# Gathering the tokens of two experts at once, with 256-column one-hot matrices on tokens split beforehand

## The reference

```
logits = h @ w_router                                  # 8 experts
top_val, top_idx = top_k(logits, 2)
gates = sum(one_hot(top_idx, 8) * softmax(top_val)[..., None], axis=-2)
out = 0
for e in range(8):
    out += gates[..., e:e+1] * ((silu(h @ w_gate[e]) * (h @ w_up[e])) @ w_down[e])
```

## Time and profile before

| | us |
|---|---|
| median of 3 runs | 1962.38 (1959.33 to 1962.86) |
| the profiled execution's own time | 1953.69 |
| its span, first to last instruction | 1951.5 |
| TensorE busy | 1850.6 |
| VectorE busy | 1636.3 |
| ScalarE busy | 1139.7 |

### The profile page before, as it was taken

How to read it: one execution, slowest core, us unless ns; L and a number is a source line. 1 busy time by engine, 2 the same in 40 slices (tenths; PEclk the granted TensorE clock), 3 DMA queues, 4 the chain that set the end, 5 groups by cost and what they waited for, 6 DMA issues and landing times.

```text
span 1951.5 us, 32205 instructions
## 1 busy us (share of the span) xinstructions
PE 1850.6 (95%) x10670; PEld 1595.1 (82%) x10670; DVE 1636.3 (84%) x2193; ACT 1139.7 (58%) x1616; POOL 36.1 (2%) x47
## 2 busy tenths in 40 slices
PE   3999999989999999999999999978899999889997
PEld 2989998867788888888888888866789997679997
DVE  6999996868998899898989898988897768897554
ACT  2445444464777777777777777753654445555443
POOL 2000000000000000000000000000000000000000
PEclk8999999999999999999999999989899999899999
DMA  9978996657899999999999999958678885855772
GB/s 323 349 270 289 385 372 182 175 178 248 266 343 359 347 357 345 356 353 348 362 336 371 330 371 331 370 181 243 189 227 283 276 262 185 231 194 188 224 226 76
DMA packets 368485, 551.26 MB, mean 282 GB/s; under 512 B 35827, under 2 KB 293110, under 8 KB 368342
## 3 DMA queue, kind: packets, MB, share of 16 engines
q1 hardware_dynamic: 365392, 547.81, 83.6%
q10 hardware_dynamic: 2118, 1.46, 0.3%
q0 software_dynamic: 832, 0.30, 0.1%
HBM read 548.38 MB, written 1.08 MB: 282 GB/s over the span
## 4 chain that ended last, share of the span: by engine, by line
PE 81%; DVE 13%; issue 3%; ACT 2%; DMA 1%; DVEq 0%; ACTq 0%; SPq 0%
PE ps L448 23%; PE ps L446 23%; PE ps L447 23%; DVE mod_acc L1768 2%; DVE units_low L441 2%; PE ps L1226 2%; PE ps L959 1%; DVE prob L1962 1%; PE ps L1101 1%; DVE x_tokens L1795 1%; DVE x_normed L1794 1%; PE ps L971 1%; DMA mod_in<-in_mod_w 1%; PE ps L806 1%; PE ps L781 1%
## 5 line engine op out<-in xcount | busy, mean ns | idle before, releaser
L441 DVE TENSOR_TENSOR units_low<-raw_units,units_high 128x1024 fp32r<-128x1024 f32 (+1 forms) x838 | 982.5, 1218 | 129.9 <-ACT units_high L437 127.2
L437 ACT ACTIVATE units_high<-raw_units 128x1024 fp32r<-128x1024 f32 (+1 forms) x838 | 846.1, 1058 | 292.0 <-PE ps L448 251.5
L446 PE MATMUL ps<-units_high,hT_high 128*128 128x512 f32 (+1 forms) x992 | 391.3, 394 | 2.7 <-DVE hT_low L2196 1.4
L448 PE MATMUL ps<-units_high,hT_low 128*128 128x512 f32 (+1 forms) x992 | 389.8, 393 | 0.0
L447 PE MATMUL ps<-units_low,hT_high 128*128 128x512 f32 (+1 forms) x992 | 386.8, 390 | 0.0
L446 PE MATMUL ps<-hT_high,units_high 128*128 128x256 f32 x1152 | 319.1, 277 | 4.2 <-DVE hT_low L1837 3.0
L447 PE MATMUL ps<-hT_low,units_high 128*128 128x256 f32 x1152 | 318.5, 276 | 0.0
L448 PE MATMUL ps<-hT_high,units_low 128*128 128x256 f32 x1152 | 318.4, 276 | 0.0
L446 PE MATMUL ps<-units_high,aT_high 128*128 128x512 f32 x632 | 255.2, 404 | 1.3 <-DVE aT_low L2048 0.6
L448 PE MATMUL ps<-units_high,aT_low 128*128 128x512 f32 x632 | 248.7, 394 | 0.0
L447 PE MATMUL ps<-units_low,aT_high 128*128 128x512 f32 x632 | 247.1, 391 | 0.0
(11 more groups left out here) (304 smaller groups left out, 1605.2 us busy)
## 6 DMA issues: line engine op xcount, KB each, us to landing
raw_units<-in_moe_w_gate SPq DMA_DIRECT2D x352, 256.0 KB, 4.6
raw_units<-in_moe_w_up SPq DMA_DIRECT2D x352, 256.0 KB, 5.8
raw_units<-in_moe_w_down SPq DMA_DIRECT2D x176, 512.0 KB, 6.1
mod_in<-in_mod_w SPq DMA_DIRECT2D x96, 512.0 KB, 6.4
mod_in<-in_w_mod SPq DMA_DIRECT2D x96, 512.0 KB, 5.6
raw_units<-in_w_gu SPq DMA_DIRECT2D x176, 256.0 KB, 3.9
raw_units<-in_w_down SPq DMA_DIRECT2D x44, 512.0 KB, 4.1
raw_units<-in_w_in SPq DMA_DIRECT2D x32, 512.0 KB, 7.6
```

The source lines that it names most:

```text
L437: eng.activation(whi[:rows, high_slot(f, n), 0:width], raw[:rows, raw_slot(f, n), 0:width], ACT.Copy).then_inc(f.hi, 1)
L441: eng.tensor_tensor(low[:rows, raw_slot(f, n), 0:width], raw[:rows, raw_slot(f, n), 0:width], whi[:rows, high_slot(f, n), 0:width].bitcast ...
L446: pe.matmul(dst, ah, bh, start=start, stop=False, **kw)
L448: return pe.matmul(dst, al, bh, start=False, stop=stop, **kw)
```

## The change

The tokens are split once, in expert 0 (ScalarE `tokens_high` and VectorE `tokens_low` at its steps 5 and 7), into `xth` and `xtl`. `hot` becomes a matrix of 256 columns in fp32r. Expert 1 and 2, 3 and 4, 5 and 6 and, at the end of expert 6, 7 and the one behind it are gathered together by `gather_pair`. Expert 0 keeps a gather of its own in float32. `hTh` and `hTl` hold two experts side by side, the even one in columns 128 to 255, the odd one in 0 to 127 (`slots`). The pair's result lies in banks 2, 3, 5 and 7 and is evicted in four parts. The bodies of the three loops hold an even and an odd expert: experts 0 and 1 are straight code, and the loop makes three turns. SP's program is unchanged. The diff, cut to its core:

```diff
-    hot = ex("gather_hot", [P, T, P])
+    hot = ex("gather_hot", [P, T, 2 * P], F32R)
+    xth = ex("tokens_high", [P, T, D], F32R)
+    xtl = ex("tokens_low", [P, T, D], F32R)
+    GATHER_BANKS = (2, 3, 5, 7)
+    def slots(odd):
+        return slice((1 - odd) * P, (2 - odd) * P)
...
     # TensorE
-        def gather(value, halves=False):
-            pe.wait_ge(s_hot, value)
-            for c in range(DC):
-                for t in range(T):
-                    last = pe.matmul(ps[:, 2 + c // 4, (c % 4) * P:(c % 4 + 1) * P], xn[:, t, c * P:(c + 1) * P],
-                                     hot[:, t, :], start=t == 0, stop=t == T - 1)
+        def gather_pair(it):
+            pe.wait_ge(s_xth, T)
+            pe.wait_ge(s_xtl, T)
+            pe.wait_ge(s_hot, it + 2 * T)
+            pe.wait_ge(s_hTe, it + 2)
+            for c in range(DC):
+                dst = ps[:, GATHER_BANKS[c // 2], (c % 2) * 2 * P:(c % 2 + 1) * 2 * P]
+                for t in range(T):
+                    pe.matmul(dst, xth[:, t, c * P:(c + 1) * P], hot[:, t, :], start=t == 0, stop=False)
+                    last = pe.matmul(dst, xtl[:, t, c * P:(c + 1) * P], hot[:, t, :], start=False, stop=t == T - 1)
+                if c % 2 == 1:
+                    last.then_inc(s_gat, 1)
...
-            swiglu(fa, N_MOE, STEPS, 1, it, first=[(s_xel, it + 2), (fa.act, STEPS + STEPS * it)],
-                   hooks={("after_T", 1): scat0, ("after_T", 2): scat1, ("after_T", 3): hot_T,
-                          ("before_T", STEPS): lambda: gather(it + 2)})
-        expert(0)
-        with pe.Fori(1, E) as it:
-            expert(it)
+            hooks = {("after_T", 1): scat0, ("after_T", 2): scat1, ("after_T", 3): hot_T}
+            if not odd:
+                hooks["before_T", STEPS] = lambda: gather_pair(it)
+            swiglu(fa, N_MOE, STEPS, 1, it, first=[(s_xel, 2 * it + (4 if odd else 2)), (fa.act, STEPS + STEPS * it)],
+                   hooks=hooks, at0=slots(odd).start)
+        expert(0, 0)
+        expert(1, 1)
+        with pe.Fori(2, E - 1, 2) as it:
+            expert(it, 0)
+            expert(it + 1, 1)
...
     # ScalarE
-        def xe_high(v):
-            ac.wait_ge(s_gat, v + 1)
-            ac.activation(hTh[:, 0:DC, 0:P], ps[:, 2:4, :].rearrange("p a (c s) -> p (a c) s", c=4), ACT.Copy)\
-                .then_inc(s_xeh, 1)
+        def xe_high(it):
+            for q in range(4):
+                ac.wait_ge(s_gat, 2 * it + 3 + q)
+                ac.activation(hTh[:, 2 * q:2 * q + 2, :].rearrange("p c s -> p (c s)"), ps[:, GATHER_BANKS[q], :],
+                              ACT.Copy).then_inc(s_xeh, 1)
+        def tokens_high(t):
+            ac.activation(xth[:, t, :], xn[:, t, :], ACT.Copy).then_inc(s_xth, 1)
+            if first:
+                hooks[5], hooks[7] = (lambda: tokens_high(0)), (lambda: tokens_high(1))
+            if not odd:
+                hooks[STEPS] = lambda: xe_high(it)
...
     # VectorE
+        def xe_low(it):
+            for q in range(4):
+                ve.wait_ge(s_xeh, 2 * it + 3 + q)
+                ve.tensor_tensor(hTl[:, 2 * q:2 * q + 2, :].rearrange("p c s -> p (c s)"), ps[:, GATHER_BANKS[q], :],
+                                 hTh[:, 2 * q:2 * q + 2, :].rearrange("p c s -> p (c s)").bitcast(F32),
+                                 ALU.subtract).then_inc(s_xel, 1)
+        def tokens_low(t):
+            ve.wait_ge(s_xth, t + 1)
+            ve.tensor_tensor(xtl[:, t, :], xn[:, t, :], xth[:, t, :].bitcast(F32), ALU.subtract).then_inc(s_xtl, 1)
+            def next_hots():
+                next_gate()
+                for t in range(T):
+                    for i in range(2):
+                        last = ve.tensor_scalar(hot[:, t, i * P:(i + 1) * P], table[:, C_IO:C_IO + P],
+                                                ranks_now[:, t, i:i + 1], None, ALU.is_equal)
+                    last.then_inc(s_hot, 1)
```

More of the change, by code:

```diff
@@ L315, in build @@
     s_vec = [sem(f"vec_in{i}") for i in range(7)]
-    s_small = [sem(f"small_in{i}") for i in range(4)]
+    s_small = [sem(f"small_in{i}") for i in range(3)]
     s_vz, s_vt, s_cols, s_sc = sem("vecs_zeroed"), sem("vecsT_in_psum"), sem("cols_ready"), sem("silu_c_ready")
@@ L1226, in gather @@
                     last = pe.matmul(ps[:, 2 + c // 4, (c % 4) * P:(c % 4 + 1) * P], xn[:, t, c * P:(c + 1) * P],
-                                     hot[:, t, :], start=t == 0, stop=t == T - 1)
-                if halves and c == DC // 2 - 1:
+                                     hot[:, t, slots(0)].bitcast(F32), start=t == 0, stop=t == T - 1)
+                if c % 4 == 3:
                     last.then_inc(s_gat, 1)
-            last.then_inc(s_gat, 1)
+        def gather_pair(it):
[10 more added lines that the diff above has]
+                    last.then_inc(s_gat, 1)
         def scatter(t, yl_value, macc_value):
@@ L1246, in _, with expert @@
         pe.wait_ge(s_hbe, 2)
-        gather(1, halves=True)
+        gather_first()
         pe.wait_ge(s_flag, 1)
         more = pe.value_load(flag[0:1, 0:1], min_val=0, max_val=1)
-        def expert(it):
+        def expert(it, odd):
             def scat0():
@@ L1275, in _ @@
         done = E + E * more
-        pe.wait_ge(s_xel, done + 2)
         pe.wait_ge(s_hTe, done + 1)
@@ L1590, in hotT_out @@
                 ac.activation(hotT[:, :], ps[:, 7, 0:S], ACT.Copy).then_inc(s_hTe, 1)
[L1592 to L1596, removed]
+            hooks = {3: hotT_out}
+            if first:
+                hooks[5], hooks[7] = (lambda: tokens_high(0)), (lambda: tokens_high(1))
+            if not odd:
+                hooks[STEPS] = lambda: xe_high(it)
+            swiglu(fa, N_MOE, STEPS, 1, it, skip=AHEAD if first else 0, hooks=hooks, opening=lambda: y_high(it))
         def y_high(done):
@@ L1602, in y_high @@
             ac.activation(yh[:, :], ps[:, 0:2, :].rearrange("p a b -> p (a b)"), ACT.Copy).then_inc(s_yh, 1)
-        expert(0)
-        with ac.Fori(1, E) as it:
-            expert(it)
+        expert(0, 0, first=True)
+        expert(1, 1)
+        with ac.Fori(2, E - 1, 2) as it:
+            expert(it, 0)
+            expert(it + 1, 1)
         with ac.If(more > 0):
-            with ac.Fori(E, 2 * E) as it:
-                expert(it)
+            with ac.Fori(E, 2 * E - 1, 2) as it:
+                expert(it, 0)
+                expert(it + 1, 1)
         with ac.Else():
@@ L1889, in swiglu @@
                     ve.wait_ge(f.silu, step0 + j + 1 + STEPS * it)
-                    if not (isinstance(it, int) and j == 0):
+                    if not (isinstance(it, int) and it == 0 and j == 0):
                         ve.wait_ge(f.tr, j + STEPS * it)
@@ L2228, in next_hot @@
+                last.then_inc(s_now, 1)
                 ve.wait_ge(s_now, it + 1)
+            def next_hots():
+                next_gate()
                 for t in range(T):
[L2230 to L2236, removed]
+                    for i in range(2):
+                        last = ve.tensor_scalar(hot[:, t, i * P:(i + 1) * P], table[:, C_IO:C_IO + P],
+                                                ranks_now[:, t, i:i + 1], None, ALU.is_equal)
+                    last.then_inc(s_hot, 1)
@@ L2238, in y_low @@
+            hooks = {1: lambda: add_scattered(0, 1 + 2 * it), 2: lambda: add_scattered(1, 2 + 2 * it),
+                     3: next_gate if odd else next_hots}
+            if first:
+                hooks[5], hooks[7] = (lambda: tokens_low(0)), (lambda: tokens_low(1))
+            if not odd:
+                hooks[STEPS] = lambda: xe_low(it)
+            swiglu(fa, N_MOE, STEPS, 1, it, skip=AHEAD if first else 0, hooks=hooks, opening=lambda: y_low(it))
         def y_low(done):
@@ L2242, in y_low @@
                              ALU.subtract).then_inc(s_yl, 1)
-        expert(0)
-        with ve.Fori(1, E) as it:
-            expert(it)
+        expert(0, 0, first=True)
+        expert(1, 1)
+        with ve.Fori(2, E - 1, 2) as it:
+            expert(it, 0)
+            expert(it + 1, 1)
         with ve.If(more > 0):
-            with ve.Fori(E, 2 * E) as it:
-                expert(it)
+            with ve.Fori(E, 2 * E - 1, 2) as it:
+                expert(it, 0)
+                expert(it + 1, 1)
         with ve.Else():
@@ L2274, in _ @@
             ve.wait_ge(s_scat, 2 * done + part + 1)
-            link(ve.scalar_tensor_tensor(out=xn[:, t, cut], in0=ps[:, 2 + 2 * t + half, :], scalar=now[:, 1, t:t + 1],
+            link(ve.scalar_tensor_tensor(out=xn[:, t, cut], in0=ps[:, 2 + 2 * t + half, :], scalar=gate_now[:, t:t + 1],
                                          in1=gate_bc[:, cut], op0=ALU.mult, op1=ALU.mult))
```

54 lines of the change are left out of this document (28 added, 26 removed).

## The result

The changed kernel takes 1972.16 us (median of five runs) where the one before takes 1962.38, 9.8 us more. The ratio, formed of the runs outside the chip's slower state alone, is 1.0067, interval 1.0050 to 1.0085, which is 13 us (10 to 17). The kernel is slower, and lies outside the predicted range. The profiled execution took 1973.2 us around a span of 1971.0.

What follows compares the result with a forecast made beforehand. TensorE's own queue was taken to bound the expert stage. Gains of 3.4 + 1.8 less 0.3 (end) and 0.3 (gathers) made 4.6 us, so 1957.8 us; range 1955 to 1962.4, 8 in 10 for 1949.5 to 1962.5.

Steps and rivals of the forecast that it cites:

- Boundaries 3 to 4 and 5 to 6: Loop's back-branches between these experts: all three doubled bodies stop for a block, leaving a gain of 0.9 us each, 1.8 together.
- 2 to 4: Sign that the forecast is right: TensorE gaps of this many us ahead of experts 4 and 6, none ahead of 2.
- D: Gathers: the new matmuls need 0.23 us each, 4 x 3.7 us more, 1972 us; chance 0.03.
- C: Branches: three engines' blocks wait for each other behind the weights; a stop of 8.1 us gives 1966; chance 0.07.
- Boundary 1 to 2: Straight code without a gather: landings keep their places, TensorE uses up the splits' lead, stall 0.1 us, gain 3.4 us.
- the backlog: Weight transfers after boundary 1 to 2: deeper at SP's stop, it can give back 3.7 us of lost delivery per boundary.
- rival B: Weights: DMA engines set the pace, TensorE gains 4.0 us of slack once, then waits; 1958.7 to 1962 us; chance 0.13.
- The end: Expert 7 to 8: VectorE stops at its branch past the second pass, the 3.56 us are lost; -0.3 us.
- The gathers: Four pair gathers, 32 matmuls each at the dense stage's pace: 3.63 us each against 3.56, a loss of 0.3 us.
- Evictions and token split: Pair boundaries: evictions hidden with 0.8 us left; expert 0, steps 5 and 7: split copies and subtractions hidden, 1.7 us late.
- Rival A: Loop branches: no stops, or stops hidden where the gather was; gain 13.5 us, 1948.9 us; chance 0.17.

Runs made afterwards that it cites:

- The shift by 30 instructions: Changed kernel with 60 waits on TensorE ahead of its loop, which put the loop's head 30 instructions later; ratio 0.9998 to the kernel before.
- the second profile: Another profiled execution of the changed kernel, unaltered; it came to the experts at 496.95 us and its expert stage took 806.7 us.
- the kernel without loops: Changed kernel with experts 1 to 7 in straight code on TensorE, ScalarE and VectorE, SyncE keeping its loop; ratio 0.9953 to the kernel before.
- the no-ops: Changed kernel with 60 empty instructions on TensorE ahead of its loop, which the compiler dropped, so the changed kernel measured again; ratio 1.0046 to the kernel before.

## Why the prediction was wrong

**The step that failed** is "Boundaries 3 to 4 and 5 to 6". It forecast a gain of 0.9 us each; experts 3 and 4 took 203.29 us and experts 5 and 6 204.39, where before they took 197.78: losses of 5.5 and 6.6. Forecast were 196.95 each (197.78, plus 0.07 for the gather, less 0.9), so these two terms are 6.3 and 7.4 us of the 15.2 by which the stage missed its forecast of 790.1. The mechanism was right: ScalarE's, VectorE's and TensorE's doubled bodies no longer stay on their engines, and their back-branches stop for a block. The size was wrong. The forecast left 2.66 us for the stop (3.56 less 0.9), and the first gap alone was that (2.68 and 2.98 us, "2 to 4"). Two things were put at nothing:

- *The next block*, 2.54 and 3.36 us. I counted one stop per branch. TensorE runs 15 instructions of the loop in 3 us and stands again for the next block. The shift by 30 instructions took this away: experts 3 and 4 went from 203.3 us (205.4 in the second profile) to 199.8, experts 5 and 6 from 204.4 to 198.7, the shorter low clock included.
- *The clock*, 3.2 and 3.4 us. I priced a gap at its length. Behind the two gaps of the changed kernel the granted clock is 0.50 for 10.2 us, in which 16 and 17 matmuls take 0.2 us more each; behind one gap it was low for 6.8 us, for 3.4 or not at all.

These are the loss: gaps and slow matmuls add up to 8.4 and 9.7 us, and the two pairs of experts stand 8.5 and 9.7 us over the kernel without loops (194.8 and 194.7). The rest of the miss, 0.5 and 0.4 us, that kernel has too.

That the latest of the three stops counts, as I took it, holds. With the second gap gone, all three together left gaps of 3.54 and 2.49 us; ScalarE's and VectorE's alone 3.59 and 2.40, TensorE's alone 2.53 and 2.62. Over the kernel without loops the three together cost 5.0 and 4.0 us, ScalarE's and VectorE's 3.4 and 2.4, TensorE's 3.7 and 2.6. What goes beyond the gaps is the clock: it was low for 3.4 us at both gaps in the first case, at neither in the second, at the first alone in the third. Such a stretch costs about 1.6 us, estimated from 0.427 and 0.229 us a matmul.

The Trainium skill, page "Runtime: NRT & Kernel Launch", section "Instruction fetch mechanics", gives TensorE room for 2048 instructions and most engines for 512. By these figures every doubled body would stay; my prediction had read the section the other way. The measurement decides: counted in the compiled program, from the loop's head to its back-branch, the bodies of two experts have 1,968 instructions on TensorE, 447 on ScalarE and 386 on VectorE, and all three stopped there (6.2, 5.2 and 5.7 us at the first). Those of one expert, 1,017, 223 and 194, didn't stop in the kernel before. SyncE's body of one, 355, did at every turn, for 5.2 us. Where between these lengths the limit lies, no run shows.

**The rivals in time.** D gave 1972 us, the time measured, but not its cause: the gathers are short (below). C gave 1966, from a single stop of 8.1 us; none in the changed kernel lasted so long (4.7 to 6.8, in its second profile up to 7.3). The stops were of ordinary length; a second one behind the first and the clock did it.

**Expert 2** took 1.4 us more than forecast. Boundary 1 to 2 gained 3.58 us (forecast 3.4), and the units then arrived late, with a gap of 0.62 us at 724.4. In the second profile expert 2 took 1.0 us more than forecast, with the no-ops 0.1. This is the backlog that I argued would hold, and a part of rival B. The runs with SyncE written out show its cause in the kernel without loops: there it costs 0.3 us per pair. That the 1.4 us here are the same wasn't tested by itself.

**The end** was forecast at a loss of 0.3 us and came at 0.45, from the stop of VectorE that was named, 6.1 us of it. One claim under it was wrong: that the kernel before passed this branch at once because it jumps over less code. The kernel before without loops jumps over the same code, and stops.

**The gathers.** A pair took TensorE 3.76 us where 3.63 was forecast; its matmuls last as long as the dense stage's, 0.28 us by their records:

```profile
L1250 PE MATMUL ps<-gather_hot,tokens_high x64: 277/280/283, 594.2 to 1201.0; 128*128 128x256 f32 x64
```

Rival D falls. **Evictions and token split** are hidden as forecast: behind a pair the first low part was ready 0.76 us before TensorE wanted it (0.8 forecast), and expert 0 grew by 0.2 us, the pair itself. **Rival A's** 13.5 us were right as the value of the edit without its loop: 13.4.

## What to carry to other kernels

Price a loop body by whether it stays on its engines, before pricing what the edit inside it saves: here a body of two experts cost 15 us a run where the saved gathers were worth 13. Count two fetches for a taken branch out of what stays, the target's block and the next, and see how many instructions run between them; writing a short loop out, or shifting its head, is cheap to try. A stop on the bounding engine cost its gap and, in most cases here, a slow clock around it. Its gap is labelled with a semaphore that it waited for, even where the work was ready 4.7 us before, so compare the time at which that work was ready.

## What was not expected of the hardware

- After a taken branch of TensorE two 16 KB blocks came in one after the other, 5.5 to 6.3 us apart in the kernels made from the changed one, and where TensorE ran only 15 instructions before the second, it stood for each. 30 instructions more ahead of a loop made the kernel 0.6% faster.
- In the loop of two with before's gathers the two blocks of a back-branch were fetched 0.7 and 0.3 us apart (893.2 and 893.9; 1096.8 and 1097.1), and the branch took 7.5 us and not 6.2. Why they came together there is open.
- Gaps of much the same length had different sequels: 3.59 us left the granted clock at 1.00 (TensorE written out), 2.53 us came with 3.4 us at 0.50 (shifted, ScalarE and VectorE written out). Two gaps, one behind the other, came with 10.2 us at 0.50 (2.68 and 2.54 us), with 6.8 (3.31 and 4.09) and with 3.4 (2.37 and 4.43).
- Straight code isn't free: the kernel before, written out, was 0.2% slower; in the stage all of it is at the one branch behind the experts.
